# The order of folds and evictions in the 64-slot expert tasks of a two-block decoder kernel, and a fourth slot of weight parts

## Chip, core and metric

The kernel runs on one core of a Trainium2 chip, as one program. The metric is device microseconds from launch to end. Engines are named as the profile names them: PE (TensorE matmul), PEld (its weight loads), DVE (VectorE), ACT (ScalarE), POOL (GpSimd), SP (SyncE, which issues the weight loads).

## What is computed

One sequence of 256 tokens of width 1024 goes through two blocks; the change touches the last part alone, a mixture of 8 experts with the 2 best of a router for each token:

```
def swiglu(t, w_gate, w_up, w_down):
    return jnp.matmul(jax.nn.silu(jnp.matmul(t, w_gate)) * jnp.matmul(t, w_up), w_down)

def moe_swiglu(h, w_router, w_gate, w_up, w_down):
    t = h.reshape(b * l, d)
    logits = jnp.matmul(t, w_router).astype(jnp.float32)
    top_val, top_idx = lax.top_k(logits, TOP_K)
    gates = jax.nn.softmax(top_val, axis=-1)
    combine = jnp.sum(jax.nn.one_hot(top_idx, N_EXPERTS, dtype=jnp.float32) * gates[..., None], axis=1)
    out = jnp.zeros((b * l, d), jnp.float32)
    for e in range(N_EXPERTS):
        y_e = swiglu(t, w_gate[e], w_up[e], w_down[e]).astype(jnp.float32)
        out = out + combine[:, e:e + 1] * y_e
```

An expert has three matrices of 1024 by 3584 in float32. A product in float32 precision is built from parts: a number is split into a high part, its value rounded to the narrower type fp32r, and a low part, the rest.

## The kernel before

Weights come in **units** of 128 partitions by 2048 numbers, 1 MB each. SP loads them in a fixed order into `raw`, a ring of six buffers: the load of unit u waits until DVE has finished unit u−6 (`lo_done`, in `moe_load`). ACT rounds a unit into `w_hi` (`split_hi`), DVE subtracts it from `raw` into `w_lo` (`split_lo`), PE multiplies both. `w_hi` and `w_lo` have three slots, so ACT waits for PE to have used unit u−3 (`unit_used`) before it rounds u.

The mixture runs as **tasks** of one expert and up to 128 token slots. With these inputs there are eight: the first and the last two have 128 slots, the five between have 64 and are the *small* tasks (`small_task` on PE, `small_hi_task` and `small_first` on ACT, `small_lo_task` on DVE; the first four in a hardware loop, the fifth written out behind it). In a small task the 64 slots' high parts and their low parts lie side by side as 128 columns of one stationary operand, so a unit takes two matmuls a column block (`mm2`: high weights, low weights) in place of three. The result then has the high tokens' rows and the low tokens' rows apart, and they must be added: the **fold**, matmuls of 64 columns against `m_fold`.

A task has 42 units. The hidden 3584 columns go in seven parts h of 512: h 0 alone, then (1, 2), (3, 4), (5, 6) as wide steps. Units 0 and 1 are the gate matrix of h 0, 2 and 3 its up matrix; 4 to 7 the gate and 8 to 11 the up of h 1 and 2, then 12 and 13 the down matrix of h 0; 14 to 17, 18 to 21 the gate and up of h 3 and 4, 22 to 25 the down of h 1 and 2; 26 to 29, 30 to 33 gate and up of h 5 and 6; 34 to 41 the rest of down. Each step goes round the engines: ACT copies the gate's sums from PSUM to `m_sg` (`gate_out`) and the up's to `m_act` (`up_out`); PE folds both into PSUM banks 0 and 1 (`fold`); ACT takes the SiLU of the first (`small_silu`), DVE the product with the second (`small_product`), ACT its high part (`small_hi`), DVE its low part (`small_lo`); then PE can multiply by the down units (`small_down`). Down sums stay in banks 4 and 5 until the end of the task, when ACT and DVE scale and add them and POOL stores the rows and gathers the tokens of the next task. `turn_rows` transposes those tokens on PE, and `tokens_hi` and `tokens_lo` split them.

All engines run in the order that is written in their part of the program, and semaphores join them. `m_sg` and `m_act` have room for two parts h, so `gate_out` of part h waits until the fold that reads the old contents is done (`m_tr`); this wait is in the code as

```
                        act.wait_ge(unit_used, used(M0 + WIDE[h // 2][0] + 3, 7 * i))
                        act.wait_ge(m_tr, HALVES * i + h)
```

and `fold` waits for both halves of its input by one semaphore, `m_mult`, before its first matmul.

Of the kernel before, what the change touches and what calls it, by code (L numbers as in the profile page):

```python
# [4 lines left out]
F32 = mybir.dt.float32  # L5
F32R = mybir.dt.float32r
# [6 lines left out]
P = 128  # L13
S = 256
# [79 lines left out]
def block_kernel(nc, I, out, stop="all"):  # L94
    ctx = ExitStack()
    with ctx:
# [36 lines left out]
        arena = sb("arena", [P, 15504])  # L133
        vec = sb("vec", [P, 3 * P])
# [106 lines left out]
        def split_hi(act, u, rounds=0, halves=(0, 1), whole=False):  # L241
# [6 lines left out]
            if whole:  # L248
                nc.scalar.activation(w_hi[:, u % SPL, :], raw[:, u % RAW, :], ACT.Copy).then_inc(hi_done, 2)  # L249
                return  # L250
# [4 lines left out]
        def split_lo(dve, u, rounds=0, halves=(0, 1), whole=False):  # L255

            if u >= LAST:
                return
            if whole:
                dve.wait_ge(hi_done, 2 * RAW * rounds + 2 * u + 2)  # L260
                nc.vector.tensor_tensor(w_lo[:, u % SPL, :], raw[:, u % RAW, :], w_hi[:, u % SPL, :].bitcast(F32),  # L261
                                        ALU.subtract).then_inc(lo_done, 1)
                return
# [329 lines left out]
        STEP_H = ((0,), (1, 2), (3, 4), (5, 6))  # L593
        m_st, m_pr, m_fold = region(3584, 512), region(6528, 512), region(7040, HALF)
# [342 lines left out]
        def _(act):  # L937
# [385 lines left out]
            if level >= 5:  # L1323
# [152 lines left out]

                def small_first(i):
# [5 lines left out]
                def small_step(i, before, j):  # L1483

                    gate_u, up_u, down_u = WIDE[j]
                    if j == 0:
                        up_out(i, 0)
                    whole_hi(i, gate_u + 2, gate_u + 3, up_u, up_u + 1)
                    gate_out(i, 2 * j + 1)
                    gate_out(i, 2 * j + 2)  # L1490
                    whole_hi(i, up_u + 2)
                    small_silu(i, j)
                    whole_hi(i, up_u + 3, up_u + 4)
                    small_hi(i, before, j)
                    whole_hi(i, up_u + 5)
                    up_out(i, 2 * j + 1)
                    up_out(i, 2 * j + 2)

                def small_hi_task(before, i, n):

                    small_step(i, before, 0)
                    whole_hi(i, 14, 15)
                    small_step(i, before, 1)
                    whole_hi(i, 24, 25, 26, 27)
                    small_step(i, before, 2)
                    whole_hi(i, 36)
                    small_silu(i, 3)
                    whole_hi(i, 37)
                    small_hi(i, before, 3)
                    whole_hi(i, 38)  # L1510
# [53 lines left out]
        def _(dve):  # L1564
# [549 lines left out]
            if level >= 5:  # L2114
# [222 lines left out]
                def whole_lo(i, *units):  # L2337

                    for u in units:
                        split_lo(dve, M0 + u, 7 * i, whole=True)  # L2340
# [15 lines left out]
                def small_step_lo(i, before, j):  # L2356

                    gate_u, up_u, down_u = WIDE[j]
                    whole_lo(i, gate_u + 2, gate_u + 3, up_u, up_u + 1, up_u + 2)
                    small_product(before, j)  # L2360
                    whole_lo(i, up_u + 3, up_u + 4)
                    small_lo(i, j)
                    whole_lo(i, up_u + 5)

                def small_lo_task(before, i, n):

                    small_step_lo(i, before, 0)
                    whole_lo(i, 14, 15)
                    small_step_lo(i, before, 1)
# [949 lines left out]
```

## Time and profile before

| | us |
|---|---|
| median of 3 runs | 1826.88 (1826.72 to 1827.2) |
| the profiled execution's own time | 1827.01 |
| its span, first to last instruction | 1825.4 |
| mean granted TensorE clock | 0.996 of full speed |

The profile is one execution. Its page gives the busy time of each engine, the span in 40 slices, the DMA queues, the chain of work that ended last, the costliest groups and the loads. Questions to the trace give groups, timelines or windows of a stretch. "Idle before" is the time an engine stood still ahead of an instruction, with the engine and line that released it. Everything before the mixture takes about the first half of the span. On the page DVE's whole-unit subtraction (L261) and ACT's whole-unit rounding (L249), which only the small tasks use, stand for 470.1 and 399.0 us.

### The profile page before, as it was taken

Reading aid. Unit: us, or ns where it says so; the run is one execution under the profiler, and the core shown is the slowest. Engines: PE = TensorE matmul, PEld = TensorE weight load, DVE = VectorE, ACT = ScalarE, POOL = GpSimd, SP = SyncE. Lnnn points to the kernel's source line nnn. Section 1 sums busy time; section 2 is a strip of 40 time slices with the busy share of each in tenths; the row PEclk is TensorE's granted clock in tenths of the full one; section 3 lists DMA queues with packets and bytes.
Section 4 is the critical chain, followed back from the end, with each engine's and each line's share of the span. In section 5 each row is a group of like instructions: output and inputs, shape, how many; then the busy total and the mean of one; then the engine's idle time right before and its main releaser. Section 6 shows DMA issues by size and latency. Waiting matters only on the chain.

```text
span 1825.4 us, 25165 instructions
## 1 busy us (share of the span) xinstructions
PE 1721.7 (94%) x8774; PEld 1416.0 (78%) x8774; DVE 1464.2 (80%) x1653; ACT 1254.8 (69%) x1490; POOL 151.0 (8%) x230
## 2 busy tenths in 40 slices
PE   9999998999999999999999888888898888999998
PEld 7888887888888899888877666666666666788886
DVE  6686785778666689685998888889888898999997
ACT  6645564556445566666777778877878787777776
POOL 2030050000000000140150000001000000000100
PEclk9999999999999999999999999999999999999999
DMA  9424569654565455506799999999999999999994
GB/s 343 148 96 139 182 179 330 231 182 152 194 194 177 161 176 177 202 24 203 275 346 383 403 384 367 412 366 411 396 371 413 365 410 400 362 399 361 411 389 183
DMA packets 176181, 515.45 MB, mean 282 GB/s; under 512 B 10964, under 2 KB 58450, under 8 KB 161634
## 3 DMA queue, kind: packets, MB, share of 16 engines
q1 hardware_dynamic: 172146, 493.08, 72.8%
q0 software_dynamic: 3808, 21.01, 3.1%
q8 instruction: 51, 0.84, 0.2%
q14 instruction: 32, 0.26, 0.0%
q10 hardware_dynamic: 144, 0.26, 0.0%
HBM read 508.01 MB, written 14.70 MB: 286 GB/s over the span
## 4 chain that ended last, share of the span: by engine, by line
PE 66%; DVE 16%; issue 9%; ACT 6%; DMA 2%; DVEq 0%; POOL 0%; ACTq 0%; POOLq 0%; SPq 0%
PE ps L274 14%; PE ps L276 13%; PE ps L275 13%; DVE w_lo L261 10%; PE ps L2801 8%; PE ps L2804 4%; PE ps L3194 4%; ACT w_hi L249 3%; PE ps L280 3%; DVE w_lo L267 2%; DMA raw<-in_w_ffn_in_dram 2%; PE ps L281 2%; PE ps L2596 1%; ACT w_hi L253 1%; ACT arena L1454 1%
## 5 line engine op out<-in xcount | busy, mean ns | idle before, releaser
L267 DVE TENSOR_TENSOR w_lo<-raw,w_hi 128x1024 fp32r<-128x1024 f32 x517 | 612.4, 1234 | 88.0 <-ACT w_hi L253 85.9
L253 ACT ACTIVATE w_hi<-raw 128x1024 fp32r<-128x1024 f32 x518 | 519.0, 1057 | 170.9 <-PE ps L276 151.9
L261 DVE TENSOR_TENSOR w_lo<-raw,w_hi 128x2048 fp32r<-128x2048 f32 x210 | 470.1, 2286 | 71.3 <-ACT w_hi L249 69.9
L249 ACT ACTIVATE w_hi<-raw 128x2048 fp32r<-128x2048 f32 x210 | 399.0, 1918 | 41.6 <-PE ps L281 38.7
L280 PE MATMUL ps<-w_hi,a 128*128 128x512 f32 x560 | 232.5, 415 | 53.0 <-DVE w_lo L261 46.7
L274 PE MATMUL ps<-w_hi,a 128*128 128x512 f32 (+1 forms) x656 | 260.3, 397 | 3.3 <-DVE w_lo L267 2.1
L276 PE MATMUL ps<-w_hi,a 128*128 128x512 f32 (+1 forms) x656 | 255.0, 389 | 0.0
L275 PE MATMUL ps<-w_lo,a 128*128 128x512 f32 (+1 forms) x656 | 254.4, 388 | 0.0
L2801 PE MATMUL ps<-a,w_hi 128*128 128x512 f32 x704 | 222.4, 397 | 6.7 <-DVE w_lo L267 6.7
L281 PE MATMUL ps<-w_lo,a 128*128 128x512 f32 x560 | 219.9, 393 | 0.0
L280 PEld LDWEIGHTS ps<-w_hi,a 128*128 128x128 f32 x560 | 105.0, 187 | 117.5 <-DVE w_lo L261 96.9
L274 PE MATMUL ps<-w_hi,a_hi 128*128 128x512 f32 (+1 forms) x440 | 170.8, 388 | 2.5 <-DVE w_lo L267 2.2
L276 PE MATMUL ps<-w_hi,a_lo 128*128 128x512 f32 (+1 forms) x440 | 169.6, 386 | 0.0
L275 PE MATMUL ps<-w_lo,a_hi 128*128 128x512 f32 (+1 forms) x440 | 169.6, 385 | 0.0
L2804 PEld LDWEIGHTS ps<-a,w_lo 128*128 128x128 f32 x704 | 132.8, 189 | 31.3
L274 PEld LDWEIGHTS ps<-w_hi,a 128*128 128x128 f32 x656 | 123.7, 189 | 31.6 <-issue 4.3
L276 PEld LDWEIGHTS ps<-w_hi,a 128*128 128x128 f32 x656 | 123.5, 188 | 25.9
L275 PEld LDWEIGHTS ps<-w_lo,a 128*128 128x128 f32 x656 | 123.8, 189 | 23.5
L280 PE MATMUL ps<-w_hi,a_hi 128*128 128x512 f32 x280 | 117.1, 418 | 23.5 <-DVE w_lo L261 12.0
L2804 PE MATMUL ps<-a,w_lo 128*128 128x256 f32 x704 | 138.8, 279 | 0.0
L281 PEld LDWEIGHTS ps<-w_lo,a 128*128 128x128 f32 x560 | 105.3, 188 | 19.0
L2801 PEld LDWEIGHTS ps<-a,w_hi 128*128 128x128 f32 x704 | 109.3, 190 | 8.3 <-DVE w_lo L267 6.9
(440 smaller groups left out, 2231.2 us busy)
## 6 DMA issues: line engine op xcount, KB each, us to landing
raw<-in_moe_w_gate_dram SPq DMA_DIRECT2D x112, 1024.0 KB, 7.1
raw<-in_moe_w_up_dram SPq DMA_DIRECT2D x112, 1024.0 KB, 8.1
raw<-in_moe_w_down_dram SPq DMA_DIRECT2D x112, 1024.0 KB, 8.3
raw<-in_ssd_w_in_dram SPq DMA_DIRECT2D x24, 1024.0 KB, 5.1
raw<-in_w_ffn_in_dram SPq DMA_DIRECT2D x22, 1024.0 KB, 5.1
raw<-in_w_in_dram SPq DMA_DIRECT2D x21, 1024.0 KB, 7.3
raw<-in_w_ffn_out_dram SPq DMA_DIRECT2D x11, 1024.0 KB, 5.0
raw<-in_dense_w_gate_dram SPq DMA_DIRECT2D x11, 1024.0 KB, 5.2
```

The source lines that it names most:

```text
L249: nc.scalar.activation(w_hi[:, u % SPL, :], raw[:, u % RAW, :], ACT.Copy).then_inc(hi_done, 2)
L253: nc.scalar.activation(w_hi[:, u % SPL, part], raw[:, u % RAW, part], ACT.Copy).then_inc(hi_done, 1)
L261: nc.vector.tensor_tensor(w_lo[:, u % SPL, :], raw[:, u % RAW, :], w_hi[:, u % SPL, :].bitcast(F32), ALU.subtract).then_inc(lo_done, 1)
L267: last = nc.vector.tensor_tensor(w_lo[:, u % SPL, part], raw[:, u % RAW, part], w_hi[:, u % SPL, part].bitcast(F32), ALU.subtract)
L274: nc.tensor.matmul(o, lh, rh, start=start, stop=False, skip_group_check=True)
L275: nc.tensor.matmul(o, lh, rl, start=False, stop=False, skip_group_check=True)
L276: return nc.tensor.matmul(o, ll, rh, start=False, stop=stop, skip_group_check=True)
L280: nc.tensor.matmul(o, l, rh, start=start, stop=False, skip_group_check=True)
L281: return nc.tensor.matmul(o, l, rl, start=False, stop=stop, skip_group_check=True)
L2801: nc.tensor.matmul(ps[bank + fc][:, :], w_hi[:, slot, cols], a0_hl[:, kc].rearrange("p a s -> p (a s)"), start=(kc == 0), stop=False, skip ...
L2804: last = nc.tensor.matmul(ps[bank + fc][:, 0:S], w_lo[:, slot, cols], a0_hi[:, kc, :], start=False, stop=(kc == DC - 1), skip_group_check= ...
L3194: last = nc.tensor.matmul(ps[n][:, at:at + HALF], paired(src, h, c), m_fold, start=True, stop=True, skip_group_check=True)
```

## The change

Three things, all in the small tasks.

1. **The fold is cut in two.** `fold(i, j, n)` has a gate part (n = 0, which waits for the gate evictions by `m_silu`) and an up part (n = 1, which waits for the up evictions by `m_mult`). Both lie earlier on PE than the gate units of the next step end: the gate part in the middle of the step's own up units, the up part behind the first two down units (in step 0 behind units 5 and 6). The waits for `m_silu` ahead of units 14 and 26 go.
2. **Evictions lie behind later roundings on ACT.** The gate evictions of a wide step come behind the roundings of its first two up units or more, the up evictions behind those of the next four units, and the roundings ahead of a SiLU are more.
3. **A fourth slot** of high and low parts, `w_hi_more` and `w_lo_more`, in a free part of the arena. `small_slot` turns units 0 to 35 of a task through slots 2, 0, 1, 3; from 36 on the old three are used, as the large tasks behind expect. `small_before(u)` is the last unit in u's slot; ACT waits for that.

The diff, cut to its core (PE's and ACT's program of a task whole, DVE's follows ACT's):

```
+        MORE_AT = 139776 + 4 * 11264
+        w_hi_more = nc.alloc_sbuf_tensor_at("w_hi_more", [P, UC], F32R, offset=MORE_AT)
+        w_lo_more = nc.alloc_sbuf_tensor_at("w_lo_more", [P, UC], F32R, offset=MORE_AT + 4 * UC)
...
+        def small_slot(u):
+            if u % MOE_UNITS >= 36:
+                return (UNIT["moe"] + u % MOE_UNITS) % SPL
+            return (2, 0, 1, 3)[u % MOE_UNITS % 4]
+
+        def small_before(u):
+            v = u - 1
+            while small_slot(v) != small_slot(u):
+                v -= 1
+            return v
...
                 def whole_hi(i, *units):
                     for u in units:
-                        split_hi(act, M0 + u, 7 * i, whole=True)
+                        act.wait_ge(raw_full[(M0 + u) % RAW], 16 * (7 * i) + 16 * ((M0 + u) // RAW + 1))
+                        act.wait_ge(unit_used, RAW * (7 * i) + (M0 + small_before(u) + 1))
+                        nc.scalar.activation(small_part(u, True), raw[:, (M0 + u) % RAW, :], ACT.Copy).then_inc(hi_done, 2)
...
                 def small_first(i):
-                    whole_hi(i, 2, 3)
+                    whole_hi(i, 2, 3, 4, 5)
                     gate_out(i, 0)
-                    whole_hi(i, 4, 5)
...
                 def small_hi_task(before, i, n):
-                    small_step(i, before, 0)
-                    whole_hi(i, 14, 15)
-                    small_step(i, before, 1)
-                    whole_hi(i, 24, 25, 26, 27)
-                    small_step(i, before, 2)
-                    whole_hi(i, 36)
+                    whole_hi(i, 6, 7)
+                    small_outs(i, 0)
+                    whole_hi(i, 8, 9, 10)
+                    small_silu(i, 0)
+                    whole_hi(i, 11)
+                    gate_out(i, 1)
+                    small_hi(i, before, 0)
+                    gate_out(i, 2)
+                    whole_hi(i, 12, 13, 14, 15)
+                    small_outs(i, 1)
+                    whole_hi(i, 16, 17)
+                    small_silu(i, 1)
+                    whole_hi(i, 18, 19)
+                    small_hi(i, before, 1)
+                    whole_hi(i, 20, 21)
+                    gate_out(i, 3)
+                    gate_out(i, 4)
+                    whole_hi(i, 22, 23, 24, 25)
+                    small_outs(i, 2)
+                    whole_hi(i, 26, 27)
+                    small_silu(i, 2)
+                    whole_hi(i, 28, 29)
+                    small_hi(i, before, 2)
+                    whole_hi(i, 30, 31, 32, 33)
+                    gate_out(i, 5)
+                    gate_out(i, 6)
+                    whole_hi(i, 34, 35, 36, 37)
+                    small_outs(i, 3)
+                    whole_hi(i, 38)
                     small_silu(i, 3)
-                    whole_hi(i, 37)
                     small_hi(i, before, 3)
-                    whole_hi(i, 38)
                     tokens_hi(i + 1, n)
                     whole_hi(i, 39, 40, 41, 42, 43)
...
+                def fold(i, j, n):
+                    src = (m_sg, m_act)[n]
+                    pe.wait_ge((m_silu, m_mult)[n], HALVES * i + STEP_H[j][-1] + 1)
+                    for k, h in enumerate(STEP_H[j]):
+                        for c in range(4):
+                            at = k * S + c * HALF
+                            last = nc.tensor.matmul(ps[n][:, at:at + HALF], paired(src, h, c), m_fold,
+                                                    start=True, stop=True, skip_group_check=True)
+                    if n:
+                        last.then_inc(m_tr, len(STEP_H[j]))
...
                 def small_task(i):
                     pe.wait_ge(m_silu, HALVES * i + 1)
+                    small_units((4, 5), 4, (2, 3), 7 * i, 2)
+                    fold(i, 0, 0)
+                    small_units((6,), 4, (2, 3), 7 * i, 2)
+                    fold(i, 0, 1)
+                    small_units((7,), 4, (2, 3), 7 * i, 2)
+                    small_units((8, 9), 8, (6, 7), 7 * i, 2)
+                    fold(i, 1, 0)
+                    small_units((10, 11), 8, (6, 7), 7 * i, 2)
+                    small_down(i, (12, 13), 12, 0)
+                    fold(i, 1, 1)
+                    small_units((14, 15, 16, 17), 14, (2, 3), 7 * i, 2)
+                    small_units((18, 19), 18, (6, 7), 7 * i, 2)
+                    fold(i, 2, 0)
+                    small_units((20, 21), 18, (6, 7), 7 * i, 2)
+                    small_down(i, (22, 23), 22, 1)
+                    fold(i, 2, 1)
+                    small_down(i, (24, 25), 22, 1)
+                    small_units((26, 27, 28, 29), 26, (2, 3), 7 * i, 2)
+                    small_units((30, 31), 30, (6, 7), 7 * i, 2)
+                    fold(i, 3, 0)
+                    small_units((32, 33), 30, (6, 7), 7 * i, 2)
+                    small_down(i, (34, 35), 34, 3)
+                    fold(i, 3, 1)
                     turn_rows(i)
+                    small_down(i, (36, 37, 38, 39, 40, 41), 34, 3)
```

On ACT, in the fifth small task (the hardware loop reads alike), the order from rounding 19 to rounding 22 was this before (L1454 is `gate_out`, here of parts h 3 and 4, L249 the rounding of a unit, L1468 the SiLU of parts h 1 and 2, the rest waits):

```order
L247 REGISTER_ALU
L249 ACTIVATE w_hi<-raw 128x2048
L1452 REGISTER_ALU
L1453 REGISTER_ALU
L1454 ACTIVATE arena<-ps 128x512 x2
L249 ACTIVATE w_hi<-raw 128x2048
L1468 ACTIVATE arena<-ps 128x512
L247 REGISTER_ALU
L249 ACTIVATE w_hi<-raw 128x2048
L245 REGISTER_ALU
L247 REGISTER_ALU
L249 ACTIVATE w_hi<-raw 128x2048
```

From rounding 15 to rounding 18 it now reads so (L1480 is `up_out` of parts h 1 and 2, L1462 the rounding, L1486 their SiLU):

```order
L1461 REGISTER_ALU
L1462 ACTIVATE w_hi_more<-raw 128x2048
L1480 ACTIVATE arena<-ps 128x512 x2
L1460 REGISTER_ALU
L1461 REGISTER_ALU
L1462 ACTIVATE w_hi<-raw 128x2048
L1461 REGISTER_ALU
L1462 ACTIVATE w_hi<-raw 128x2048
L1485 REGISTER_ALU
L1486 ACTIVATE arena<-ps 128x512
L1461 REGISTER_ALU
L1462 ACTIVATE w_hi<-raw 128x2048
```

The SiLU of parts h 1 and 2, behind rounding 20 and the gate evictions of parts h 3 and 4 before, now stands behind rounding 17 and the up evictions of its own parts; the gate evictions of h 3 and 4 come later, behind rounding 21. Unit 15 goes into the fourth slot (`w_hi_more`).

On PE, at the end of gate unit 17, the fold of parts h 1 and 2 stood whole before up unit 18 (L280 and L281 are the two matmuls of `mm2`, L3194 the fold):

```order
L280 MATMUL ps<-w_hi,a 128x512
L281 MATMUL ps<-w_lo,a 128x512
L3194 MATMUL ps<-arena 128x64 x16
L3177 REGISTER_ALU
L280 MATMUL ps<-w_hi,a 128x512
L281 MATMUL ps<-w_lo,a 128x512
L280 MATMUL ps<-w_hi,a 128x512
L281 MATMUL ps<-w_lo,a 128x512
```

Now its gate part lies between up units 9 and 10 of its own step (L275 and L276 are `mm2`, L3226 the fold, L3222 the wait ahead of it),

```order
L275 MATMUL ps<-w_hi,a 128x512
L276 MATMUL ps<-w_lo,a 128x512
L3222 REGISTER_ALU
L3226 MATMUL ps<-arena 128x64 x8
L3203 REGISTER_ALU
L275 MATMUL ps<-w_hi,a 128x512
L276 MATMUL ps<-w_lo,a 128x512
```

and its up part between down unit 13 and gate unit 14:

```order
L275 MATMUL ps<-w_hi,a_hi 128x512
L276 MATMUL ps<-w_lo,a_hi 128x512
L3226 MATMUL ps<-arena 128x64 x8
L3203 REGISTER_ALU
L275 MATMUL ps<-w_hi,a 128x512
L276 MATMUL ps<-w_lo,a 128x512
L275 MATMUL ps<-w_hi,a 128x512
```

The sixteen matmuls became eight and eight, 8 units and 4 units ahead of where they stood.

## Rows read from the trace of the kernel before

**Rows 1.** The page, part 1: busy us, share of the span, instructions.

```profile
PE 1721.7 (94%) x8774; PEld 1416.0 (78%) x8774; DVE 1464.2 (80%) x1653; ACT 1254.8 (69%) x1490; POOL 151.0 (8%) x230
```

**Rows 2.** Timeline of POOL: result stores; start us, us, engine, line, what.

```profile
1118.61 0.56 POOL L789 DMA_DIRECT2D result_rows<-arena  x1 [106.98 <-DVE arena L2385]
...
1580.32 0.56 POOL L789 DMA_DIRECT2D result_rows<-arena  x1 [104.38 <-DVE arena L2385]
```

**Rows 3.** Windows: us, each engine's busy time, granted clock, DMA share, GB/s.

```profile
core 0: us, PE busy (x) PEld busy (x) DVE busy (x) ACT busy (x) POOL busy (x), PEclk, DMA share, GB/s
1215.30:1330.60 115.30, 100.70 (x457) 74.46 (x457) 100.12 (x57) 91.53 (x69) 4.96 (x3) 1.00 0.99 390
1219.30:1239.30 20.00, 16.46 (x63) 11.39 (x64) 19.96 (x15) 16.76 (x12) 0.56 (x1) 1.00 1.02 374
1239.30:1285.30 46.00, 40.39 (x185) 30.10 (x185) 38.68 (x21) 36.60 (x29) 4.41 (x2) 1.00 1.02 423
1285.30:1293.30 8.00, 6.57 (x27) 4.35 (x25) 7.86 (x5) 7.15 (x7) 0.00 (x0) 1.00 0.91 333
1293.30:1315.30 22.00, 20.43 (x98) 15.31 (x96) 17.57 (x9) 16.22 (x12) 0.00 (x0) 1.00 1.02 424
1315.30:1330.60 15.30, 13.14 (x74) 10.94 (x75) 12.06 (x9) 10.80 (x11) 0.00 (x0) 1.00 0.95 349
```

**Rows 4.** Groups of DVE, 1215.3 to 1330.6: busy us, mean ns | idle before.

```profile
L261 DVE TENSOR_TENSOR w_lo<-raw,w_hi 128x2048 fp32r<-128x2048 f32 x43 | 96.5, 2287 | 14.3 <-ACT w_hi L249 13.9
```

**Rows 5.** Groups of ACT, same stretch.

```profile
L249 ACT ACTIVATE w_hi<-raw 128x2048 fp32r<-128x2048 f32 x43 | 81.8, 1918 | 8.5 <-PE ps L281 6.2 <-DMA raw<-in_moe_w_up_dram 2.2
L1454 ACT ACTIVATE arena<-ps 128x512 f32<-128x512 f32 x7 | 3.9, 597 | 9.2 <-PE ps L3194 9.1
...
L1468 ACT ACTIVATE arena<-ps 128x512 f32<-128x512 f32 (+1 forms) x4 | 2.2, 546 | 3.7 <-PE ps L3194 3.7
```

**Rows 6.** Timeline of PE: one unit's first and last record, fold, next.

```profile
1272.55 0.50 PE L280 MATMUL ps<-w_hi,a 128*128 128x512 f32 x1
...
1274.27 0.39 PE L281 MATMUL ps<-w_lo,a 128*128 128x512 f32 x1
1274.50 3.87 PE L3194 MATMUL ps<-arena 128*128 128x64 f32 x32
1278.18 0.48 PE L280 MATMUL ps<-w_hi,a 128*128 128x512 f32 x1
```

**Rows 7.** Timeline of ACT around that fold, in brackets idle before and releaser.

```profile
1278.41 1.09 ACT L1454 ACTIVATE arena<-ps 128x512 f32<-128x512 f32 x2 [3.43 <-PE ps L3194]
1279.38 1.92 ACT L249 ACTIVATE w_hi<-raw 128x2048 fp32r<-128x2048 f32 x1
```

**Rows 8.** Timeline of DVE: the waits at the four steps, and a full run.

```profile
1253.64 2.29 DVE L261 TENSOR_TENSOR w_lo<-raw,w_hi 128x2048 fp32r<-128x2048 f32 x1 [2.38 <-ACT w_hi L249]
...
1281.33 2.29 DVE L261 TENSOR_TENSOR w_lo<-raw,w_hi 128x2048 fp32r<-128x2048 f32 x1 [4.03 <-ACT w_hi L249]
...
1289.14 20.14 DVE L261 TENSOR_TENSOR w_lo<-raw,w_hi 128x2048 fp32r<-128x2048 f32 x9
1313.71 2.29 DVE L261 TENSOR_TENSOR w_lo<-raw,w_hi 128x2048 fp32r<-128x2048 f32 x1 [4.43 <-ACT w_hi L249]
...
1328.22 0.69 DVE L2346 TENSOR_TENSOR arena<-arena,ps 128x512 f32<-128x512 f32 x1 [1.97 <-ACT arena L1468]
1330.03 2.29 DVE L261 TENSOR_TENSOR w_lo<-raw,w_hi 128x2048 fp32r<-128x2048 f32 x1 [1.12 <-ACT w_hi L249]
```

**Rows 9.** Source line of the expert loads: issue to landing.

```profile
DMA to landing us min/median/max: 4.9/8.6/11.5
```

**Rows 10.** DMA of the period 1215.3 to 1330.6.

```profile
DMA packets 10872, 44.96 MB, mean 390 GB/s; under 512 B 703, under 2 KB 703, under 8 KB 9079
```

More of the change, by code:

```diff
@@ L239, in block_kernel, with split_hi @@
         LAST = [UNIT["ffn0"], UNIT["pool"], UNIT["ffn1"], UNIT["dt"], UNIT["moe"], UNIT["moe"] + 1000][level]
-        def split_hi(act, u, rounds=0, halves=(0, 1), whole=False):
+        def split_hi(act, u, rounds=0, halves=(0, 1)):
             if u >= LAST:
@@ L247, in split_hi @@
                 act.wait_ge(unit_used, RAW * rounds + u - SPL + 1)
-            if whole:
-                nc.scalar.activation(w_hi[:, u % SPL, :], raw[:, u % RAW, :], ACT.Copy).then_inc(hi_done, 2)
-                return
             for n in halves:
@@ L253, in split_hi, with split_lo @@
                 nc.scalar.activation(w_hi[:, u % SPL, part], raw[:, u % RAW, part], ACT.Copy).then_inc(hi_done, 1)
-        def split_lo(dve, u, rounds=0, halves=(0, 1), whole=False):
+        def split_lo(dve, u, rounds=0, halves=(0, 1)):
             if u >= LAST:
[L258 to L262, printed above, removed]
                 return
@@ L3169, in task, with small_units @@
                         down_last(i)
-                def small_units(u, banks, rounds, nk, tokens=None):
-                    cols_n = UC // nk
-                    for q in range(DC // nk):
+                def small_units(units, first, banks, rounds, nk, tokens=None):
+                    n = UC // nk
+                    for u in units:
+                        q = u - first
                         if tokens is not None:
                             pe.wait_ge(m_alo, 2 * tokens + q + 3)
-                        pe.wait_ge(lo_done, RAW * rounds + (M0 + u + q + 1))
-                        slot = (M0 + u + q) % SPL
+                        pe.wait_ge(lo_done, RAW * rounds + (M0 + u + 1))
+                        hi, lo = small_part(u, True), small_part(u, False)
@@ L3179, in small_units @@
                         for k in range(nk):
                             kc = nk * q + k
-                            for half in range(cols_n // WB):
-                                cols = slice(k * cols_n + half * WB, k * cols_n + (half + 1) * WB)
-                                last = mm2(ps[banks[half]][:, :], a0_hi[:, kc, 0:P], w_hi[:, slot, cols],
-                                           w_lo[:, slot, cols], kc == 0, kc == DC - 1)
+                            for half in range(n // WB):
+                                cols = slice(k * n + half * WB, k * n + (half + 1) * WB)
+                                last = mm2(ps[banks[half]][:, :], a0_hi[:, kc, 0:P], hi[:, cols], lo[:, cols],
+                                           kc == 0, kc == DC - 1)
@@ L3198, in small_down, with small_head @@
[L3198 to L3212 removed]
+                def small_head(i):
+                    small_units((0, 1), 0, (2,), 7 * i, 4, i)
+                    small_units((2, 3), 2, (6,), 7 * i, 4)
+                    pe.wait_ge(m_yhi, 2 * i)
@@ new lines, in small_down @@
+                def small_down(i, units, base, h0):
+                    for u in units:
+                        h, b = h0 + (u - base) // 2, (u - base) % 2
+                        if b == 0:
+                            pe.wait_ge(m_plo, HALVES * i + h + 1)
+                        pe.wait_ge(lo_done, RAW * (7 * i) + (M0 + u + 1))
+                        hi, lo = small_part(u, True), small_part(u, False)
+                        by_half = u == MOE_UNITS - 1
+                        order = [(k, half) for half in range(2) for k in range(2)] if by_half else [
+                            (k, half) for k in range(2) for half in range(2)]
+                        for k, half in order:
+                            cols = slice(k * D + half * 512, k * D + (half + 1) * 512)
+                            mm = mm2(ps[4 + half][:, :], pair(h)[:, 2 * b + k, :], hi[:, cols], lo[:, cols],
+                                     u == 12 and k == 0, by_half and k == 1)
+                            if by_half and k and half == 0:
+                                mm.then_inc(m_half, 1)
+                        mm.then_inc(unit_used, 1)
```

109 lines of the change are left out of this document (26 added, 83 removed).

## The prediction

> **What bounds the kernel now.** The page's busy shares come first [rows 1]: PE 94%, DVE 80%, ACT 69%, so over the whole program no engine has all of the time, and the shares mix stages. The change touches the 64-slot tasks alone, so I looked for their period. The stores of their results are five, the first issued at 1118.61 and the last at 1580.32 us [rows 2]: four periods in 461.7 us, 115.4 us each. Five tasks are 577 us of the 1825.4 us span.
>
> Then one period by stretches [rows 3]. In 115.3 us PE is busy 100.7, DVE 100.1, ACT 91.5, and the DMA engines have a share of 0.99 at 390 GB/s. Three numbers close together, so the question is which waits last. The DVE groups answer for DVE [rows 4]: 43 subtractions of a whole unit, and 14.3 us of idle time ahead of them, 13.9 of it until ACT had rounded the unit. ACT in turn [rows 5] sat idle 9.1 us ahead of the gate evictions and 3.7 ahead of the SiLUs, both until the fold on PE (L3194) was done. The timelines show it as one event. At 1274.50 PE begins 32 records of folds, 3.87 us [rows 6]. ACT starts the two gate evictions at 1278.41 after 3.43 us idle, then rounds the next unit at 1279.38 [rows 7]. DVE starts that unit at 1281.33 after 4.03 us idle [rows 8]. The other steps do the same: 2.38, 4.43 and 1.97 us [rows 8]. This is the stall that bounds the period: the gate parts of the next step may not be evicted before the old ones are folded, so a fold of both halves stands on PE while ACT and DVE have nothing.
>
> The transfers are the second limit, and it is near. While DVE runs without a large stall, 1239.3 to 1285.3, they move 423 GB/s at a share of 1.02, and again 424 GB/s from 1293.3 to 1315.3 [rows 3]. Behind the stalls they fall to 333 and 349 GB/s at 0.91 and 0.95 [rows 3]: a load goes out only when DVE has finished the unit six before, so a late DVE empties the queue. A load lands 4.9 us after its issue at the least, 8.6 at the median [rows 9]. A period moves 44.96 MB [rows 10].
>
> **The change, part by part.** Nothing is added or removed in number: still 42 loads, 42 roundings, 42 subtractions and 56 fold matmuls a task; SP's and POOL's instructions stay.
>
> *Folds ahead of the next step's gate.* Each fold is cut in a gate half and an up half, 1.9 us each on PE for the wide steps (half of 3.87, rows 6). They now lie behind units 5, 6, 9, 13, 19, 23, 31 and 35, so when the evictions at units 17 and 29 are due, their fold was done units before. The three large waits of ACT go, and with them DVE's idle 2.38, 4.03 and 4.43 us.
>
> *The new waits on PE.* A gate half waits for gate evictions that stand behind roundings 11, 21 and 33 on ACT; in step 0 the second stands behind the product's high part too. I walked this with the rows' durations: rounding 1.92, two evictions 1.09, subtraction 2.2 (nine in 20.14 us, rows 8), fold half 1.9, a unit on PE 1.95 at most (1272.55 to 1274.50, rows 6). At step 0 PE waits some 2 us before fold half (1, gate) and is 2 to 3 us late for the next units; at the up half behind unit 13 it waits 1 to 2 more. PE's own work is 42 × 1.95 + 13.6 for the folds + 1 for the transposes, 97 us at most, so in 109 us it has 12 to lose and the walk spends about 8.
>
> *The fourth slot.* With three slots ACT rounds unit u when PE has used u−3, with four when it has used u−4. In the walk PE finishes unit 14 about 4.9 us after subtraction 15 begins and unit 15 at 6.8; rounding 18 is due at 5.5 to 5.9. With three slots it would wait a microsecond, with four it does not. That is the cover for the fold waits; without it each wide step gives back 1 to 1.5 us. The slot lies in the arena, in SBUF; rounding into it should cost what the other slots cost, 1918 ns [rows 5]; a different time is excluded by no row, but only its like is in the trace. Units 36 to 2 still turn in three slots.
>
> *The end of a task* is not cured. Put the end of rounding 37 at 0. Evictions to 1.1; rounding 38 and the up half of fold 3 side by side to 3.0; SiLU to 3.6; subtraction 38 from 3.0 to 5.2; product 0.6, high part 0.6, low part 0.6, to about 7.1; token roundings beside it; rounding 39 to 9.0. Subtraction 39 begins at 9.0 where transfers alone would have it at 5.0: 4 us late. DVE idles some 2 to 3 us in it, about what it idles there now (1.97 and 1.12, rows 8).
>
> *What is late next.* DVE's work is 98 us a period (100.1 less one subtraction, since the window holds 43). With 4 us of idle time left it needs 102. The transfers need 44.96 MB at 423.5 GB/s, 106.2 us. So the transfers become the bound, and only part of the 15 us of DVE's idle time comes back. Two losses are added. From 1219.3 to 1239.3, where the result is stored and the next rows fetched, they move 374 GB/s at a full share [rows 3]; against 423.5 that is 0.99 MB, 2.3 us. Bounds: nothing (if it is only the late DVE) and 2.3; I take 2.3, since the store and the fetch stay. The late end of the task costs between nothing and what follows a 4.03 us stall now, 8 us at 333 GB/s, which is 1.7 us; I take 0.6, since in the walk the load behind unit 39 goes out 4 us before the one ahead of it has landed, less than the 4.9 of the quickest landing. Sum: 106.2 + 2.3 + 0.6 = 109.1 us, 6.3 less than 115.4. Five tasks: **31.5 us**.
>
> The profiled execution took 1827.01 us with its span of 1825.4; the median of three is 1826.88. 1827.0 − 31.5 = **1795.5 us**, and against the median the same to 0.1.
>
> The Trainium skill speaks against this (DMA: Bandwidth & Descriptors, "Where 436 GB/s comes from"): for transfers from HBM to SBUF a limit of about 358 GB/s for a core binds. By that rule, as an estimate, 44.96 MB would take 125.6 us, more than the period now takes, and nothing could be won; this trace disagrees with it, with 423 GB/s for 46 us. The same section gives the fabric's ceiling as 435 GB/s, by which the floor would be 103.4 us.
>
> **Rivals.**
> *A, the share is the limit.* The DMA engines show 0.99 already and 1.02 when full. If the turnover stretches stay as slow as they are because of what is moved there, only the gap in share is won: 3% of 115.4, 3.4 us a task, 17 us: 1810. For it: 374 GB/s at share 1.02. Against it: 349 GB/s comes with 0.95 and right behind DVE's stalls.
> *B, no gain.* Transfers bind altogether and the stalls are hidden behind them: 1827. The Trainium skill's rule of 358 GB/s is this case. Against it: SP waits for DVE before loads, and 333 GB/s follows a stall.
> *C, slower.* The fold waits close a ring: PE waits for an eviction on ACT, ACT's eviction stands behind a rounding that waits for PE. If the fourth slot does not cover it, each of the seven half folds that wait costs an eviction pair and a rounding, 1.09 + 1.92, 21 us a task in place of the 14.3 now: 6.7 more, 34 us in all: 1861. It decides once PE's waits pass 115.4 − 97 = 18 us a task. For it: in three places PE now waits for ACT where it did not. Against it: the walk finds 8 us.
> *D, more than forecast.* The store costs nothing and the rate holds throughout: 106.2 a task, 9.2 × 5 = 46 us: 1781.
>
> **How the numbers follow.** Forecast 0.65, A 0.17, B 0.04, C 0.07, D 0.07. A measurement of this kernel tells a change of 0.2% (3.7 us) from none. Faster: forecast, A and D, 0.89; same: B, 0.04; slower: C, 0.07. The range goes from 1784, where store and late end together cost half a microsecond, to 1813, a little above A, which also takes in a forecast that gives back half of its gain; C, B and part of D stay outside, under 0.2.
>
> **What the profile after would show.** Stores of results about 109 us apart; PE's folds in records of 16, none followed by an ACT idle over 1 us; no DVE idle of 4 us at the wide steps, but many short ones until ACT, and ACT's until a load has landed; 410 GB/s or more over a period; share 1.0 or above. DVE still idle 2 to 3 us between units 38 and 39. Wrong, if DVE's waits end with ACT waiting for PE at units 12 to 18 (C), if the period is 112 us with 349 to 374 GB/s still between tasks (A), or if loads wait for DVE while ACT does not wait for loads.

## The result, and the profile after

The changed kernel takes 1787.57 us (median of 4 runs, 1785.73 to 1789.17), the one before 1827.04 beside it (4 runs): a ratio of 0.9781, 95% interval 0.9768 to 0.9794, 39.5 us less. The forecast was 1795.5 in a range of 1784 to 1813: the direction and the bound that took over are right, the gain is 8 us larger than the sum gave. One slow run, 1823.19 us of the kernel with 64 rows below, is left out of its median and ratio.

The profiled execution took 1786.82 us with a span of 1785.1, 40.3 less than before. POOL's timeline gives the first and the last store of a small task's result, as in [rows 2]:

```profile
1110.29 0.56 POOL L805 DMA_DIRECT2D result_rows<-arena  x1 [97.93 <-DVE arena L2410]
...
1540.05 0.56 POOL L805 DMA_DIRECT2D result_rows<-arena  x1 [90.64 <-DVE arena L2410]
```

Four periods in 429.8 us are 107.4 us each, where it was 115.4. From the store of task 0 to that of the first small task (999.63 to 1110.29, before 998.91 to 1118.61) it is 9.0 us less. So 32 us come from four periods and 9 from the first.

One period after, from the windows (busy times as in [rows 3], then granted clock, DMA share, GB/s), and its DMA totals, as in [rows 10]:

```profile
1217.11:1324.60 107.49, 98.37 (x457) 78.13 (x456) 100.09 (x57) 91.22 (x69) 12.47 (x3) 0.97 1.02 422
```

```profile
DMA packets 11021, 45.35 MB, mean 422 GB/s; under 512 B 717, under 2 KB 717, under 8 KB 9229
```

DVE's work is the same 100.1 us, PE's and ACT's too; the transfers run at 422 GB/s over the whole period, not over parts of it. The groups of DVE and ACT in that period stand against [rows 4, 5]:

```profile
L2368 DVE TENSOR_TENSOR w_lo<-raw,w_hi 128x2048 fp32r<-128x2048 f32 x34 | 76.6, 2284 | 6.2 <-ACT w_hi L1462 6.1
L1462 ACT ACTIVATE w_hi<-raw 128x2048 fp32r<-128x2048 f32 x33 | 62.7, 1915 | 10.5 <-PE ps L276 5.9 <-DMA raw<-in_moe_w_up_dram 2.4 <-DMA raw<-in_moe_w_gate_dram 2.0
...
L2368 DVE TENSOR_TENSOR w_lo_more<-raw,w_hi_more 128x2048 fp32r<-128x2048 f32 x9 | 20.5, 2283 | 0.4 <-ACT w_hi_more L1462 0.4
...
L1462 ACT ACTIVATE w_hi_more<-raw 128x2048 fp32r<-128x2048 f32 x10 | 19.1, 1912 | 3.3 <-DMA raw<-in_moe_w_gate_dram 1.6 <-DMA raw<-in_moe_w_up_dram 1.4 <-DMA raw<-in_moe_w_down_dram 0.4
```

DVE's idle time ahead of subtractions fell from 14.3 to 6.6 us. No eviction waits for a fold any more. ACT now waits for loads, 7.8 us (2.4 + 2.0 in the first row, 3.4 in the last) where it was 2.2; its wait for PE to free a slot is 5.9, where it was 6.2. The fourth slot costs what the others cost, 1912 ns and 2283 ns. A load lands later, because more of them are queued; from the source line of the loads, as in [rows 9]:

```profile
DMA to landing us min/median/max: 6.2/9.8/11.5
```

DVE's timeline has its longest wait of the period behind fold half (2, gate), and the end of the task behind it, as in [rows 8]:

```profile
1271.11 6.90 DVE L2368 TENSOR_TENSOR w_lo<-raw,w_hi 128x2048 fp32r<-128x2048 f32 x3 [1.34 <-ACT w_hi L1462]
...
1309.19 0.69 DVE L2381 TENSOR_TENSOR a_hi<-arena,a_hi 128x512 fp32r<-128x512 f32 x1 [0.83 <-ACT a_hi L1492]
...
1311.46 11.10 DVE L2368 TENSOR_TENSOR w_lo<-raw,w_hi 128x2048 fp32r<-128x2048 f32 x5 [0.70 <-ACT w_hi L1462]
```

### The profile page after: what moved, and what is told of

Its sections match the earlier page's. It is cut to its first block, busy times and chain, and to the rows that moved or that the text cites. A ratio compares the mean times of both kernels' runs of the same rounds, so it can differ in the third digit from the quotient of the medians.

```text
span 1785.1 us, 25176 instructions
## 1 busy us (share of the span) xinstructions
PE 1709.8 (96%) x8774; PEld 1432.4 (80%) x8774; DVE 1465.9 (82%) x1653; ACT 1254.0 (70%) x1490; POOL 188.0 (11%) x230
## 4 chain that ended last, share of the span: by engine, by line
PE 64%; DVE 14%; DMA 10%; issue 7%; ACT 5%; POOL 0%; DVEq 0%; ACTq 0%; SPq 0%; POOLq 0%
PE ps L269 14%; PE ps L271 14%; PE ps L270 14%; PE ps L2826 8%; DVE w_lo L2368 6%; DMA raw<-in_moe_w_gate_dram 5%; PE ps L2829 4%; DMA raw<-in_moe_w_up_dram 3%; DVE w_lo L262 3%; DMA raw<-in_w_ffn_in_dram 2%; DVE w_lo_more L2368 2%; ACT w_hi L1462 2%; PE ps L275 2%; PE ps L276 2%; PE ps L3226 1%
## 5 line engine op out<-in xcount | busy, mean ns | idle before, releaser
L2368 DVE TENSOR_TENSOR w_lo<-raw,w_hi 128x2048 fp32r<-128x2048 f32 x165 | 372.3, 2286 | 32.8 <-ACT w_hi L1462 31.6
L1462 ACT ACTIVATE w_hi<-raw 128x2048 fp32r<-128x2048 f32 x165 | 313.7, 1915 | 52.4 <-PE ps L276 23.5
L275 PE MATMUL ps<-w_hi,a 128*128 128x512 f32 x420 | 177.3, 422 | 14.6 <-DVE w_lo L2368 12.9
L276 PE MATMUL ps<-w_lo,a 128*128 128x512 f32 x420 | 170.6, 406 | 0.0
L2829 PEld LDWEIGHTS ps<-a,w_lo 128*128 128x128 f32 x704 | 133.3, 189 | 31.5
L269 PEld LDWEIGHTS ps<-w_hi,a 128*128 128x128 f32 x656 | 123.3, 188 | 31.6 <-issue 4.3
L271 PEld LDWEIGHTS ps<-w_hi,a 128*128 128x128 f32 x656 | 123.1, 188 | 25.7
L270 PEld LDWEIGHTS ps<-w_lo,a 128*128 128x128 f32 x656 | 123.3, 188 | 23.4
L275 PEld LDWEIGHTS ps<-w_hi,a 128*128 128x128 f32 x420 | 83.1, 198 | 45.8 <-DVE w_lo L2368 28.9
L1174 ACT ACTIVATE arena<-ps 128x256 f32<-128x256 f32 x88 | 28.9, 381 | 109.5 <-PE ps L2829 109.5
L275 PE MATMUL ps<-w_hi,a_hi 128*128 128x512 f32 x240 | 96.2, 401 | 8.3 <-DVE w_lo L2368 7.5
```

Of the source, the lines that this page charges most:

```text
L269: nc.tensor.matmul(o, lh, rh, start=start, stop=False, skip_group_check=True)
L270: nc.tensor.matmul(o, lh, rl, start=False, stop=False, skip_group_check=True)
L271: return nc.tensor.matmul(o, ll, rh, start=False, stop=stop, skip_group_check=True)
L275: nc.tensor.matmul(o, l, rh, start=start, stop=False, skip_group_check=True)
L276: return nc.tensor.matmul(o, l, rl, start=False, stop=stop, skip_group_check=True)
L1174: last = nc.scalar.activation(dst[:, fc, :], ps[bank + fc][:, S:2 * S], ACT.Copy)
```

## The experiments

Theory T, in the texts below, is the prediction's: loads set the pace of a small task now, and DVE has about 5 us to spare in it. Theory M, formed after the first four runs, is about what ran first: whatever stops PE for longer than the slots allow comes out as idle time of DVE. All medians are in us, with the ratio to the kernel before run beside it. The period is the mean of the four between the five stores of small tasks in the profiled execution.

| kernel | median | ratio, 95% interval | period |
|---|---|---|---|
| changed kernel | 1787.57 | 0.9781, 0.9768 to 0.9794 | 107.4 |
| new order, three slots | 1828.56 | 0.9999, 0.9984 to 1.0014 | 115.8 |
| old order, four slots | 1827.56 | 0.9999, 0.9990 to 1.0007 | 115.4 |
| whole folds, four slots | 1785.68 | 0.9759, 0.9747 to 0.9772 | 107.6 |
| gate parts a unit later | 1786.91 | 0.9765, 0.9753 to 0.9778 | 107.7 |
| whole folds, three slots | 1803.33 | 0.9866, 0.9848 to 0.9883 | 110.6 |
| changed, 3/4 of the loads | 1756.50 | 0.9611, 0.9592 to 0.9630 | 101.5 |
| before, 3/4 of the loads | 1828.23 | 0.9998, 0.9988 to 1.0007 | 115.4 |
| whole folds, 3/4 of the loads | 1761.94 | 0.9633, 0.9616 to 0.9650 | 102.4 |
| gate parts later, 3/4 of the loads | 1756.40 | 0.9601, 0.9583 to 0.9618 | 101.4 |
| DVE with 4.4 us more a task | 1789.47 | 0.9784, 0.9770 to 0.9797 | 108.1 |
| DVE with 13.2 us more a task | 1829.60 | 1.0007, 0.9997 to 1.0016 | 116.2 |
| 64 rows stored and fetched | 1784.50 | 0.9770, 0.9756 to 0.9785 | 108.7 |

### Order and slot apart

**The order without the slot.**

```
-            if u % MOE_UNITS >= 36:
-                return (UNIT["moe"] + u % MOE_UNITS) % SPL
-            return (2, 0, 1, 3)[u % MOE_UNITS % 4]
+            return (UNIT["moe"] + u % MOE_UNITS) % SPL
```

> The changed kernel with the new order, but the small tasks turn in the old three slots (small_slot always gives the unit number modulo 3). Theory T (loads set the pace of a small task, 107.4 us, and DVE has some 5 us of slack a task): the missing slot makes ACT wait a microsecond or so at each wide step, which the slack takes up: 1787 to 1795 us. Rival C' (the slot is what makes the new order work): PE's waits at the folds come back to DVE, half of the gain or more is lost: 1805 us or more, with DVE idle over 2 us at the wide steps.

Nothing is left of the gain. Theory T failed here; the rival held, and more strongly than it said. The timeline of DVE in this kernel shows its waits over 1 us in one period:

```profile
1261.75 8.90 DVE L2366 TENSOR_TENSOR w_lo<-raw,w_hi 128x2048 fp32r<-128x2048 f32 x4 [3.34 <-ACT w_hi L1460]
1272.63 2.29 DVE L2366 TENSOR_TENSOR w_lo<-raw,w_hi 128x2048 fp32r<-128x2048 f32 x1 [1.98 <-ACT w_hi L1460]
...
1288.97 8.90 DVE L2366 TENSOR_TENSOR w_lo<-raw,w_hi 128x2048 fp32r<-128x2048 f32 x4 [1.84 <-ACT w_hi L1460]
1299.73 2.29 DVE L2366 TENSOR_TENSOR w_lo<-raw,w_hi 128x2048 fp32r<-128x2048 f32 x1 [1.86 <-ACT w_hi L1460]
...
1321.08 8.90 DVE L2366 TENSOR_TENSOR w_lo<-raw,w_hi 128x2048 fp32r<-128x2048 f32 x4 [1.98 <-ACT w_hi L1460]
```

and the group of ACT's roundings what it waited for:

```profile
L1460 ACT ACTIVATE w_hi<-raw 128x2048 fp32r<-128x2048 f32 x43 | 81.2, 1914 | 22.3 <-PE ps L276 21.4 <-DMA raw<-in_moe_w_up_dram 0.7
```

The three stops of 2.4, 4.0 and 4.4 us behind whole folds [rows 8] became five of 1.8 to 3.3 behind half folds: 13.5 us ahead of subtractions in this period, 14.3 before. ACT no longer waits for a fold to evict; it waits 21.4 us for PE to free a slot.

A part of this is PE's clock. The four periods are 112.81, 114.59, 116.56 and 119.38 us long, and the granted clock is 1.00, 0.99, 0.97 and 0.94 in them. The first and the last, as windows:

```profile
1119.43:1232.24 112.81, 98.03 (x457) 75.00 (x456) 100.27 (x57) 90.72 (x69) 3.30 (x3) 1.00 1.00 400
1463.39:1582.77 119.38, 103.50 (x459) 80.69 (x459) 101.03 (x57) 91.02 (x71) 2.97 (x4) 0.94 0.99 384
```

In the first, DVE's five stops are 1.97, 1.76, 1.83, 1.86 and 1.97 us. The first stop of a period grows to 3.34 us in the period above and to 4.99 in the next, where PE ran at the lower clock just before it:

```profile
1378.46 8.90 DVE L2366 TENSOR_TENSOR w_lo<-raw,w_hi 128x2048 fp32r<-128x2048 f32 x4 [4.99 <-ACT w_hi L1460]
```

So the stops at full clock cost 5.4 us a task against the changed kernel (112.8 to 107.4), and the other 3.0 of the 8.4 came with the falls of the clock. No run takes the falls away alone, but the twelve runs fit this: the quickest, 1821.51 us, had a mean clock of 0.990, the slowest, 1836.35, one of 0.983.

**The slot without the order**: `small_slot`, `small_part` and the two arrays in the kernel before, folds and evictions as they stood.

> The kernel before with the fourth slot alone; folds and evictions stand where they stood. Theory T: the gate evictions still wait for a whole fold on PE, ACT can only be one unit further ahead, and that unit stands behind the evictions in its queue: 1815 to 1828 us. Rival C': with the slot ACT's work ahead covers the folds, 1800 us or less.

Theory T held. DVE stands where it stood, 2.57, 4.45 and 4.42 us for 2.38, 4.03 and 4.43 [rows 8]:

```profile
1251.96 2.29 DVE L2366 TENSOR_TENSOR w_lo<-raw,w_hi 128x2048 fp32r<-128x2048 f32 x1 [2.57 <-ACT w_hi L1469]
...
1279.65 2.29 DVE L2366 TENSOR_TENSOR w_lo<-raw,w_hi 128x2048 fp32r<-128x2048 f32 x1 [4.45 <-ACT w_hi L1469]
1312.01 2.29 DVE L2366 TENSOR_TENSOR w_lo<-raw,w_hi 128x2048 fp32r<-128x2048 f32 x1 [4.42 <-ACT w_hi L1469]
```

So the new order with its cut folds, and the slot, are each worth nothing alone that these runs can tell from none, and together they are worth 2.2%. Two waits stood at the same place: the eviction's for the fold, and the slot's for PE behind the fold. That is not the last word on the order: with whole folds it has a worth of its own, below.

**Whole folds**, at the place of their up part:

```
                     small_units((8, 9), 8, (6, 7), 7 * i, 2)
-                    fold(i, 1, 0)
                     small_units((10, 11), 8, (6, 7), 7 * i, 2)
                     small_down(i, (12, 13), 12, 0)
+                    fold(i, 1, 0)
                     fold(i, 1, 1)
```

and so in the other wide steps, with four slots

> The changed kernel with the folds of the three wide steps whole, at the place of their up part (behind units 13, 23, 35). Theory T: the gate evictions of the next step are still far behind, PE is busy 3.7 us in one piece with a fourth slot to cover it, and SiLU comes 1.9 us later: 1787 to 1793 us, and PE no longer waits for gate evictions, so the granted clock is nearer to 1. Rival (the cut in two is what counts): 1800 us or more.

and with three

> The new order with whole folds behind units 13, 23 and 35, in three slots. With three slots ACT may round unit u only when PE has used u-3, so whatever holds PE longer than about 0.6 us holds ACT and then DVE. Theory M (margin: every stop of PE past it comes out as DVE idle): without the gate part's wait for ACT there is one stop of 3.7 us a wide step in place of two of 1.9 with a wait each; DVE idles 9 to 12 us a task, not 13.4: 1800 to 1822 us. Rival (in three slots the order is worthless as such): 1825 us or more.

With four slots the cut in two is worth nothing here. With three, the whole fold wins 25 us that the cut fold does not, so the order alone, with whole folds, is worth 1.3% without the slot. Its DVE group shows 8.8 us of idle time, a little under the 9 to 12 expected, where the cut fold's shows 13.5.

```profile
L2366 DVE TENSOR_TENSOR w_lo<-raw,w_hi 128x2048 fp32r<-128x2048 f32 x43 | 96.5, 2288 | 8.8 <-ACT w_hi L1460 8.6
```

The direction is theory M's. The margin is an estimate from the rows: subtraction u−3 begins at 0 and ends at 2.2, PE has used the unit at 4.15 (1.95 more), and rounding u must begin by 6.6 − 1.9 = 4.7 to be ready for subtraction u. PE may be half a microsecond late with three slots, and 2.2 more with four. A gate half costs PE its 1.9 us and the wait for the evictions in front of it; a whole fold at the later place waits for less (0 in this kernel's trace, 4.4 to 5.3 us a period with cut folds) and stops PE once. But the clock is in the 25 us too: with whole folds it is 1.00 in all four periods. Against the one period of the cut folds at full clock, 112.8 us, this kernel's 110.6 is 2.2 us less, which is the part of the stops; the other 3.0 of the 5.2 us a task go with the clock. The wide step's one stop in this kernel is 2.42 and 2.83 us on DVE:

```profile
1261.76 2.29 DVE L2366 TENSOR_TENSOR w_lo<-raw,w_hi 128x2048 fp32r<-128x2048 f32 x1 [2.42 <-ACT w_hi L1460]
...
1288.39 2.29 DVE L2366 TENSOR_TENSOR w_lo<-raw,w_hi 128x2048 fp32r<-128x2048 f32 x1 [2.83 <-ACT w_hi L1460]
```

### What sets the pace now

**Loads cut to three quarters**, in the changed kernel and in the one before:

```
+                    n = src.shape[-1] * 3 // 4
-                    sp.dma_start(raw[:, (M0 + u) % RAW, :].rearrange("p (k n) -> p k n", k=src.shape[-2]),
-                                 src).then_inc(raw_full[(M0 + u) % RAW], 16)
+                    sp.dma_start(raw[:, (M0 + u) % RAW, :].rearrange("p (k n) -> p k n", k=src.shape[-2])[:, :, 0:n],
+                                 src[:, :, 0:n]).then_inc(raw_full[(M0 + u) % RAW], 16)
```

> The changed kernel with every expert load of tasks 1 to 7 cut to three quarters of its columns (768 KB in place of 1 MB; the last quarter of each row piece is left out, so a part of the products is computed from old buffer contents). All else stands. Theory T: loads set the pace, so the period of a small task falls from 107.4 us to what DVE needs, its 98 us of work and 2 to 5 us of waits: 100 to 103, and the kernel to 1750 to 1775 us. Rival E (an engine chain already sets the pace and loads merely keep up): period 106 to 108, 1780 to 1790 us.

> The same cut of the loads in the kernel before (the same part of the computation changed). Theory T: there the folds' waits set the pace, so the period stays within 113 to 115.5 us and the kernel within 1812 to 1828 us. If loads had set the pace there too (the rival by which nothing could have been won), it falls below 1800 us.

Both as theory T had it. The same cut takes 31 us from the changed kernel and nothing from the old one. The windows of one period, after and before:

```profile
1210.00:1311.00 101.00, 95.08 (x457) 75.66 (x457) 99.22 (x57) 89.90 (x69) 18.54 (x3) 1.00 0.95 337
```

```profile
1217.00:1332.00 115.00, 100.38 (x457) 74.17 (x456) 99.82 (x56) 91.12 (x69) 5.37 (x3) 1.00 0.87 296
```

In the changed kernel the DMA share is still 0.95 at 337 GB/s, so the share alone does not tell how near the transfers are to their limit. With less to load, the changed kernel has DVE busy 99.2 of 101.0 us and is bound by it; the old one still has its 13.5 us of idle time:

```profile
L2369 DVE TENSOR_TENSOR w_lo<-raw,w_hi 128x2048 fp32r<-128x2048 f32 x34 | 76.1, 2286 | 0.9 <-ACT w_hi L1463 0.9
```

```profile
L261 DVE TENSOR_TENSOR w_lo<-raw,w_hi 128x2048 fp32r<-128x2048 f32 x42 | 94.0, 2287 | 13.5 <-ACT w_hi L249 13.2
```

**More work for DVE**, `nc.vector.tensor_reduce(stat[:, ...], raw[:, (M0 + u) % RAW, :], AX.X, ALU.add)` ahead of two or of six of the subtractions of a task.

> The changed kernel with two more instructions of about 2.2 us on DVE in each small task (a sum over a loaded unit ahead of subtractions 13 and 27, its result unused). Theory T: DVE has 107.4 - 102 = about 5 us to spare a task, so 4.4 us more change the time by less than 6 us in all: 1786 to 1793 us. Rival E (DVE or a chain through it is the bound): 4.4 x 5 = 22 us more, 1810.

> Six such instructions a task, 13.2 us. Theory T: DVE's 98 + 13.2 + 2 to 4 us of waits, 113 to 115 us, pass the loads' 107.4, so a period grows by 6 to 8 us and the kernel to 1817 to 1828 us. If the time grew by the full 13.2 x 5 = 66 us (1853), DVE had nothing to spare.

4.4 us more a task moved the median by 1.9 us in all, inside the two kernels' intervals. 13.2 us more moved it by 42, 8.4 a task, so about 5 of the 13.2 were free. Its granted clock was 0.981, the changed kernel's 0.989, so a part of the 42 may be PE's. With the two additions DVE is busy 101.87 of 107.00 us, and the groups show each addition at 2280 ns:

```profile
1220.00:1327.00 107.00, 98.78 (x454) 77.22 (x452) 101.87 (x58) 89.07 (x67) 11.41 (x3) 0.97 1.02 413
```

```profile
L2369 DVE TENSOR_REDUCE stat<-raw 128x1 f32<-128x2048 f32 x2 | 4.6, 2280 | 0.0
```

**The cut folds when loads hide nothing.**

> Whole folds and four slots, with the loads cut to three quarters, so that loads no longer hide what the cut in two is worth (a part of the products is computed from old buffer contents, as in the other kernels with cut loads). Theory M: four slots leave a margin of about 2.8 us, a whole fold takes 3.7, so up to 1 us shows at each of three steps: period 101 to 104 us, 1756 to 1772 us. Rival (the cut is worth nothing even then): 1757 within 3.

> Gate parts one unit later, four slots, loads cut to three quarters (the same part of the computation changed). Theory M: DVE has nearly no idle time left with the plain cut loads (0.9 us ahead of subtractions), so nothing is to be won: 1753 to 1761 us. Rival P (PE's waits for gate evictions cost time once loads do not hide them): 1752 us or less.

Whole folds cost 5.4 us here, one microsecond a task, though the two intervals overlap a little. The waits show where: ACT stands at the SiLU, for the later fold.

```profile
ACT arena L1487 <- PE ps L3227: 5.0, 3, 3.4
```

So the cut has a small worth once loads do not cover it; the place of the gate part has none.

**Gate parts one unit later** (behind units 10, 20 and 32) in the full kernel:

> The changed kernel with each gate part one unit later (behind units 10, 20, 32), so that PE has work while ACT evicts. Theory T: PE's waits of 1.5 us ahead of the gate folds and the stretches at half the granted clock behind them go, mean clock above 0.995, and the time does not change by more than 3 us, as loads set the pace: 1784 to 1789 us. Rival P (PE's lost clock costs time): 5 us or more faster.

The time is as expected, the clock is not: 0.988 on average, no better than 0.989. PE now has no wait for gate evictions, but it is a unit late and waits for the up evictions instead:

```profile
1249.66 2.37 PE L3226 MATMUL ps<-arena 128*128 128x64 f32 x16 [2.08 <-ACT arena L1480]
```

### A version that should have been faster

**64 rows.** POOL stores and fetches 128 rows a task, and a small task has 64. Its one loop over tasks became four, with row counts of their own:

```
+                for first, end, n_in, n_out in ((0, 1, HALF, P), (1, n_small, HALF, HALF), (n_small, n_next, P, HALF),
+                                                (n_next, n_last, P, P)):
+                    with pool.Fori(first, end) as i:
+                        turn_over(i, n_in, n_out)
```

> The changed kernel, with POOL moving only the 64 rows that a small task has: results of small tasks are stored as 64 rows, and tokens of small tasks are fetched as 64 rows, 256 KB less each. Theory T: loads and these transfers share one limit of 423 GB/s, so 0.52 MB less is 1.2 us a small task, 6 us in all: 1779 to 1784 us where the changed kernel takes 1787. Rival: the limit is not in the sum of bytes (POOL's transfers lie beside the loads, or the loads' own queue is the bound): 1785 us or more.

Neither theory is shown: the median of 1784.50 lies between the two numbers, 6 us less would be a ratio of 0.9751, just outside its interval, and the interval overlaps that of the changed kernel. The five runs lie in two groups, 1783.15, 1784.20 and 1784.50 against 1790.50 and 1790.67. The profiled one is the 1790.50, and its four periods are uneven, from the stores:

```profile
1108.84 0.59 POOL L808 DMA_DIRECT2D result_rows<-arena  x1 [98.45 <-DVE arena L2418]
1220.80 0.57 POOL L808 DMA_DIRECT2D result_rows<-arena  x1 [86.71 <-DVE arena L2418]
1328.16 0.56 POOL L808 DMA_DIRECT2D result_rows<-arena  x1 [89.63 <-DVE arena L2418]
1434.32 0.56 POOL L808 DMA_DIRECT2D result_rows<-arena  x1 [80.92 <-DVE arena L2418]
1543.79 0.56 POOL L808 DMA_DIRECT2D result_rows<-arena  x1 [86.65 <-DVE arena L2418]
```

111.96, 107.36, 106.16 and 109.47 us; the third is the shortest of any kernel with full loads. In the first, and some us beyond it, the transfers themselves were slower at a full share:

```profile
1140.00:1220.00 80.00, 71.38 (x314) 55.86 (x313) 69.02 (x41) 62.23 (x47) 0.00 (x0) 0.94 1.02 387
```

That is 387 GB/s, where the stretch from 1225 to 1320 has 419 at the same share. In the changed kernel's trace no 40 us of the small tasks are below 397 GB/s. What slowed them is not shown. The period grew by 4.5 us against the changed kernel's mean, as it should if transfers set the pace. By estimate, 85 us at 387 in place of 420 GB/s lose 6.7 us, about what lies between the two groups of runs. So the rate of a full queue is not a constant either, and the worth of the 64 rows stays open.

## Why the prediction was right, and where its sum was off

- **What bounded the kernel before** was right. Cutting the loads there changed nothing, and rivals A and B, by which the transfers already had all or most of the time, fall with it: the turnover stretches that moved 349 and 374 GB/s [rows 3] now move 413 and 422 (1306.0 to 1324.5 and 1217 to 1240). One reading of mine was wrong on the way: the stretches at 423 and 424 GB/s are not free of large stalls. They hold DVE's stops of 2.38 and 4.03 us, and of 4.43 [rows 8]. The transfers ran on through the stops and fell only behind them, since loads already issued were still under way. The rate taken from them stands.
- **The transfers as the next bound** was right: 422 GB/s at 1.02, and the two experiments with cut loads.
- **The term of store and fetch**, 2.3 us a task, was mis-sized, and it is the main miss. I had bounds of nothing and 2.3 and took the upper one, on the ground that store and fetch stay. They stayed, and the slow stretch went with DVE's large stops, so it came of late loads more than of the store. **The late end of a task**, 0.6 us, was mis-sized as well. The two were 2.9 us above the 106.2 of the bytes; measured is 107.4, so 1.2 is left above that term. About 0.5 of it is bytes: over the four periods 180.63 MB were moved, 45.16 a period, not 44.96. The rest is the mean rate, 420 GB/s and not 423.5. The gain is 1.7 us a task larger than the sum's, and 8.5 over five, the 8 us between 31.5 and 39.5. By the size of the gain this is rival D's end (9.2 us a task), of which 8.0 came true.
- **DVE's need of 102 us**, 5 to spare, was right: with cut loads 101.0 to 101.5, and about 5 of 13.2 us free.
- **PE's new waits** were forecast as about 8 us of lateness; the fold halves waited 4.9 us a period in the trace, for ACT.
- **The worth of the fourth slot** was wrong. The step said that without it "each wide step gives back 1 to 1.5 us". Three slots gave back everything, 8.4 us a task: 5.4 at full clock, and 3.0 with falls of PE's clock, which the walk did not have at all. I had walked one rounding at the transfers' pace, where it has half a microsecond to spare and more after each load. Without the slot nearly two stops a wide step, five a task, pass to DVE, and DVE with its stops becomes the pace. The ring of rival C was therefore real: with three slots it decides, and it puts the kernel at the old time, not at 1861. I priced it at 21 us of waits a task; DVE's idle time in it is 13.5.
- **The end of the task** idles DVE for 0.83 and 0.70 us in the shown period, less than the 2 to 3 forecast.

## What to carry to other kernels

When a producer waits for a consumer's slot and for an ordering of the consumer's other work, each wait alone can hide behind the other: test both together before one is written off, and test each in more than one form: the order was worth nothing in three slots with cut folds and 25 us with whole ones. Ask of every wait put on PE how late PE may be before a slot is missed; here it was, by estimate, 0.5 us with three slots and 2.7 with four, and a stop of 1.9 us plus a wait is past the first and within or near the second. With so little room a fall of PE's clock passes on too. Transfers that fall off right behind a stall are a consequence of it; take the rate from the stretches in which the queue stayed full for the whole period, and do not trust the DMA share alone.

## What the runs showed of the hardware

**Rate.** The kernel, on one core, took 45.35 MB at 422 GB/s for 107.5 us, and the Trainium skill's limit of about 358 GB/s for a core (DMA: Bandwidth & Descriptors, "Where 436 GB/s comes from") does not hold here.

**Clock.** Behind the 1.49 us in which PE waited for the evictions, the granted clock fell from 1.00 to 0.50, which is 1.2 of 2.4 GHz, and PE was at it for about 3 us. Windows of the changed kernel:

```profile
1264.00:1266.00 2.00, 2.00 (x15) 2.00 (x15) 1.57 (x2) 1.82 (x2) 0.00 (x0) 0.74 1.00 422
1266.00:1268.00 2.00, 2.00 (x5) 1.55 (x6) 2.00 (x2) 1.33 (x1) 0.00 (x0) 0.50 1.02 430
1268.00:1270.00 2.00, 2.00 (x9) 1.63 (x8) 1.76 (x1) 0.84 (x1) 0.00 (x0) 0.90 0.97 408
```

```profile
1263.49 2.50 PE L3226 MATMUL ps<-arena 128*128 128x64 f32 x16 [1.49 <-ACT arena L1472]
```

The waits of 1.17 and 1.37 us earlier in the same task had no such fall behind them, and one of 0.84 us later in it had:

```profile
1293.23 2.10 PE L3226 MATMUL ps<-arena 128*128 128x64 f32 x16 [0.84 <-ACT arena L1472]
```

```profile
1296.00:1298.00 2.00, 2.00 (x6) 1.54 (x6) 2.00 (x2) 1.07 (x1) 0.00 (x0) 0.50 1.01 426
```

So the length of one wait does not tell whether the clock falls. With four slots the falls cost nothing that the runs can tell: with whole folds PE hardly waits (0.3 us a period), the mean clock is 0.994 in the profiled execution, and the time is the same within the intervals. With three slots and cut folds 3.0 us a task came with them.

**POOL starved by DVE.** POOL's cast of one number for each partition, behind the store of a small task, took 0.2 to 2.2 us in the kernel before. In the changed one it took 7.5 to 14.8 behind four of the five stores, and 0.4 behind the last, where a large task follows:

```profile
1331.82 14.79 POOL L795 CAST slot_idx<-slot_io 128x1 int32 x1 [6.64 <-DMA result_rows<-arena]
```

In that stretch DVE runs subtractions with hardly a gap. The Trainium skill (SBUF — State Buffer, "Who interferes with whom") says that DVE and GpSimd share a pair of SBUF ports under an exclusive lock, and that a DVE instruction with two SBUF inputs, as these subtractions have, contends with a GpSimd instruction that reads SBUF. The trace fits it; no run here shows that the lock, and nothing else, is the cause. The fetch behind the cast came later for it, and the fetched tokens are needed only behind unit 35, so it should have cost nothing here.
